# One chunk of 256 tokens instead of two of 128 in the chunked mLSTM of a three-block network

## The reference

```python
def mlstm_scan(q, k, v, li, lf, state):
    """true C = C*exp(m)."""
    ...
    def step(carry, inp):
        C, n, m = carry
        qx, kx, vx, lix, lfx = inp
        b = jnp.cumsum(lfx, axis=-1)
        dmat = b[..., :, None] - b[..., None, :] + lix[..., None, :]
        dmat = jnp.where(lower, dmat, -jnp.inf)
        inter = b + m[..., None]
        m_t = jnp.maximum(inter, jnp.max(dmat, axis=-1))
        w = jnp.exp(dmat - m_t[..., None])
        a = jnp.exp(inter - m_t)
        s = jnp.einsum("bhtd,bhsd->bhts", qx, kx) * w
        num = a[..., None] * jnp.einsum("bhtd,bhde->bhte", qx, C) + jnp.einsum("bhts,bhse->bhte", s, vx)
        den = a * jnp.einsum("bhtd,bhd->bht", qx, n) + jnp.sum(s, axis=-1)
        h = num / jnp.maximum(jnp.abs(den), jnp.exp(-m_t))[..., None]
        ...  # decay the state, add this chunk's keys times values
        return (C_new, n_new, m_new), h

def merge(y_fourier, h, o, g_f, g_m, head_g, w_four, w_mproj, w_out):
    hn = rmsnorm_2(h.transpose(0, 2, 1, 3), head_g.reshape(M_HEADS, M_HEAD_DIM)).reshape(B, T, M_WIDTH)
    hm = jax.nn.sigmoid(o) * hn
    y = jax.nn.sigmoid(g_f) * (y_fourier @ w_four) + jax.nn.sigmoid(g_m) * (hm @ w_mproj)
    return y @ w_out
```

## Time and profile before

| | us |
|---|---|
| median of 3 runs | 2546.47 (2544.3 to 2546.47) |
| the profiled execution | 2544.8, of it the span 2543.4 |
| TensorE busy | 2069.5 (81%) |
| DVE, ACT busy | 1008.2, 747.2 |
| the stage of the four heads | 1689 to 1886 |

### The profile page before, as it was taken

The page is one execution under the profiler, slowest core; times in us unless marked ns, Lnnn a source line. Parts: engine busy times, 40 slices in busy tenths (PEclk is TensorE's granted clock), DMA queues, the critical chain, the costliest instruction groups (busy, mean ns, idle before and its releaser), DMA issues.

```text
span 2543.4 us, 29602 instructions
## 1 busy us (share of the span) xinstructions
PE 2069.5 (81%) x12430; PEld 1378.3 (54%) x12430; DVE 1008.2 (40%) x1791; ACT 747.2 (29%) x1197; POOL 24.6 (1%) x21
## 2 busy tenths in 40 slices
PE   5888767777778787877688899778789899889895
PEld 3534313323333333323343798577778799676694
DVE  2533321112212212223442545665655545553475
ACT  4333320101111111122110444423344544533344
POOL 0000000000000000000000000000000000000000
PEclk8979888899898899888898999888889899899897
DMA  9848799999999999999999555152144455340430
GB/s 359 330 165 316 295 399 414 410 409 410 410 405 411 411 411 411 408 409 405 385 409 403 167 185 172 50 165 69 57 143 164 133 183 179 107 137 1 149 108 16
DMA packets 228243, 672.08 MB, mean 264 GB/s; under 512 B 11520, under 2 KB 134528, under 8 KB 187792
## 3 DMA queue, kind: packets, MB, share of 16 engines
q1 hardware_dynamic: 228112, 670.21, 69.3%
HBM read 669.12 MB, written 1.05 MB: 263 GB/s over the span
## 4 chain that ended last, share of the span: by engine, by line
PE 54%; DMA 28%; DVE 11%; ACT 5%; issue 2%; POOL 0%; SPq 0%; DVEq 0%; ACTq 0%
DMA ring<-in_w 22%; PE pb L227 12%; PE pb L228 12%; PE pb L229 12%; DMA ring<-in_w_a 3%; PE pb L1481 3%; PE pb L1504 2%; DVE WB L310 2%; PE pb L578 2%; DMA ring<-in_w_in 1%; DMA ring<-in_w_mod 1%; ACT WB L304 1%; PE pb L1465 1%; DVE tmpT L414 1%; PE pb L755 1%
## 5 line engine op out<-in xcount | busy, mean ns | idle before, releaser
L310 DVE TENSOR_TENSOR WB<-ring,WB 128x1024 fp32r<-128x1024 f32 (+3 forms) x370 | 425.2, 1191 | 506.3 <-ACT WB L304 505.8
L304 ACT ACTIVATE WB<-ring 128x1024 fp32r<-128x1024 f32 (+3 forms) x370 | 361.2, 1025 | 814.0 <-DMA ring<-in_w_a 466.8
L227 PE MATMUL pb<-HH,WB 128*128 128x256 f32 (+1 forms) x1680 | 504.3, 300 | 20.7 <-DVE big L2348 8.0
L228 PE MATMUL pb<-HL,WB 128*128 128x256 f32 (+1 forms) x1680 | 491.6, 293 | 0.0
L229 PE MATMUL pb<-HH,WB 128*128 128x256 f32 (+1 forms) x1680 | 490.8, 292 | 0.0
L1481 PE MATMUL pb<-ring,big 128*32 128x512 f32 x2048 | 300.1, 679 | 145.0 <-DMA ring<-in_w 127.7
L227 PEld LDWEIGHTS pb<-HH,WB 128*128 128x128 f32 x1680 | 338.0, 201 | 47.8 <-issue 20.7
L228 PEld LDWEIGHTS pb<-HL,WB 128*128 128x128 f32 x1680 | 337.9, 201 | 2.4 <-issue 2.2
L229 PEld LDWEIGHTS pb<-HH,WB 128*128 128x128 f32 x1680 | 336.9, 201 | 0.0
L1481 PEld LDWEIGHTS pb<-ring,big 128*32 128x32 f32 x2048 | 47.1, 114 | 365.6 <-DMA ring<-in_w 272.5
L1504 PE MATMUL pb<-ring,big 128*32 128x512 f32 x1024 | 174.2, 667 | 59.1 <-DMA ring<-in_w 51.0
(11 more groups left out here) (420 smaller groups left out, 2043.8 us busy)
## 6 DMA issues: line engine op xcount, KB each, us to landing
ring<-in_w SPq DMA_DIRECT2D x384, 1024.0 KB, 14.4
ring<-in_w_a SPq DMA_DIRECT2D x66, 1024.0 KB, 11.8
ring<-in_w_in SPq DMA_DIRECT2D x38, 1024.0 KB, 7.5
ring<-in_w_b SPq DMA_DIRECT2D x33, 1024.0 KB, 5.1
ring<-in_w_ada SPq DMA_DIRECT2D x32, 1024.0 KB, 6.3
ring<-in_w_mod SPq DMA_DIRECT2D x24, 1024.0 KB, 8.3
ring<-in_w_out SPq DMA_DIRECT2D x8, 1024.0 KB, 5.2
ring<-in_b_w_in SPq DMA_DIRECT2D x8, 1024.0 KB, 6.4
```

The lines of the kernel that those rows point to most:

```text
L227: pe.matmul(o, l[0], r[0], start=start, stop=False)
L228: pe.matmul(o, l[0], r[1], start=False, stop=False)
L304: act.activation(WB[:, c % 2, 0, x:y], flat[:, x:y], ACT.Copy).then_inc(*A(("high", c, z)))
L310: dve.tensor_tensor(WB[:, c % 2, 1, x:y], flat[:, x:y], WB[:, c % 2, 0, x:y].bitcast(F32), ALU.subtract).then_inc(*V(("low", c, z), *([("f ...
```

## The change

The 256 tokens of a head are one chunk. Per head the exponents of both directions are two matmuls of 36 rows and 256 columns (`M`), and two more (`A`) make the factor of the old state, which DVE multiplies into q (`qa`, two operations of 512 columns) ahead of the output matmuls. The scores (8 matmuls of 128x128) are made once and serve both directions: for the two blocks on the diagonal in both, and for the other two in one each. An output bank collects weighed scores times values and `qa` times the state as one sum in PSUM, 14 matmuls of 128x257 per head in four banks. Keys are no longer transposed or weighed, and the state isn't updated, decayed or kept. `finish` transposes into one bank in its third step instead of its fifth, there is one `hs` instead of two, and the denominators work straight from PSUM. `mlstm` has 6 steps instead of 8, and each is paired with 4 steps of `proj`. The silu of k stands ahead of the O units. In the gates, scans run over 256 tokens; the state's decay and the rows for it go.

Of the diff, the functions `mlstm` are shown by their new lines alone, since the old ones stand above.

```diff
+                    dve.tensor_tensor_scan(in_time(MM_c, d), in_time(rr_c, d), in_time(rr_c, d), 0.0, ALU.max, ALU.max).then_inc(*V())
+                dve.wait_ge(*last("v"))
+                for d in range(2):
+                    dve.tensor_tensor(small[seg[d], 0:1], at_end(bb_c, d), at_end(MM_c, d), ALU.add).then_inc(*V())
+                    dve.tensor_scalar(qw_c[seg[d], :], rr_c[seg[d], :], at_end(MM_c, d), None, ALU.subtract).then_inc(
+                        *V(*([("gate_rows_c",)] if d else [])))
...
         def gates_columns():
             q_ = gate_rows()
-            pe.wait_ge(*at("dd"))
-            pe.matmul(PB[2][:, 0:8], ones[0:36, :], q_[0][:, 0:8], start=True, stop=True).then_inc(*P(("dec",)))
+            pe.wait_ge(*at("gate_exps"))
             x = 0
-            for qi, ap in enumerate((q_[3], q_[6], q_[4], q_[5])):
...
         def finish(h):
-            for _ in range(4):
-                yield
+            yield
+            yield
             for i in range(2):
                 pe.wait_ge(*at("hs_gated", h, i))
-                pe.wait_ge(*(at("C", h + 1, 1, i) if h < 3 else at("hm_out", 2, i)))
+                if i == 0:
+                    pe.wait_ge(*at("wT", min(h + 1, 3)))
                 for f in range(2):
-                    e = pe.transpose(PB[6 + i][:, 128 * f:128 * f + 128], hs[h % 2][:, i, 128 * f:128 * f + 128], ident)
-                e.then_inc(*P(("hs_turned", h, i)))
-            yield
+                    e = pe.transpose(PB[3][:, 256 * f + 128 * i:256 * f + 128 * i + 128], hs[:, i, 128 * f:128 * f + 128], ident)
+            e.then_inc(*P(("hs_turned", h)))
 
...
         def mlstm(h):
             fin = finish(h - 1) if h else iter(())
+            q_, k_, v_ = qTm[h % 2], kTm[h % 2], va[h % 2]
+
+            def rows_of(d):
+                return k("m8")[0:36, 4 * d + h:4 * d + h + 1].to_broadcast([36, 128])
+
+            pe.wait_ge(*(at("hm_out", h - 2) if h >= 2 else at("gc_out")))
+            for d in range(2):
+                e = pe.matmul(PB[3][:, 256 * d:256 * d + 256], rows_of(d), MM[:, :], start=True, stop=True)
+            e.then_inc(*P(("M", h)))
+            pe.wait_ge(*(at("den", h - 1, 1, 1) if h else at("gc_out")))
+            for d in range(2):
+                e = pe.matmul(PB[4][:, 256 * d:256 * d + 256], rows_of(d), qA[:, :], start=True, stop=True)
+            e.then_inc(*P(("A", h)))
             pe.wait_ge(*at("ready", h))
+            for x, (s_, t) in enumerate(BLOCKS):
+                for f in range(2):
+                    e = pe.matmul(PB[2][:, 128 * x:128 * x + 128], k_[:, f, 128 * s_:128 * s_ + 128], q_[:, f, 128 * t:128 * t + 128],
+                                  start=f == 0, stop=f == 1)
+            e.then_inc(*P(("S", h)))
+            steps(fin, 1)
+            yield
+            steps(fin, 1)
+            yield
+            steps(fin, 1)
+            yield
+            for d in range(2):
+                for t in range(2):
+                    o = PB[OB[2 * d + t]][:, 0:257]
+                    if (d, t) == (0, 0):
+                        pe.wait_ge(*at("sT", h))
+                    if h:
+                        pe.wait_ge(*at("den", h - 1, d, t))
+                    elif (d, t) == (0, 1):
+                        pe.wait_ge(*at("y_low", 3))
+                    pe.matmul(o, wT[:, d, 128 * t:128 * t + 128], v_[:, t, :], start=True, stop=False)
+                    if t != d:
+                        pe.matmul(o, wT[:, d, 256:384], v_[:, d, :], start=False, stop=False)
+                    for f in range(2):
+                        e = pe.matmul(o, qa[:, f, d, 128 * t:128 * t + 128], Cc(h, d, f), start=False, stop=f == 1)
+                    e.then_inc(*P(("num", h, d, t)))
+                yield
+            yield
 
...
+            def silu(x, names):
+                x = x.rearrange("p a b -> p (a b)")
+                act.activation(x, x, ACT.Silu).then_inc(*A(*names))
+
...
         def mlstm(h):
             fin = finish(h - 1) if h else iter(())
+            steps(fin, 1)
+            yield
+            act.wait_ge(*at("wT0", h))
+            for d in range(2):
+                act.activation(wT[:, d, 256:384], PB[3][:, 256 * d + 128 * (1 - d):256 * d + 128 * (1 - d) + 128], ACT.Exp,
+                               bias=gc[:, 0, d, 4 * d + h:4 * d + h + 1], scale=-1.0).then_inc(*A())
+            for d in range(2):
+                for t in range(2):
+                    w = wT[:, d, 128 * t:128 * t + 128]
+                    act.activation(w, w, ACT.Exp, bias=gc[:, 0, t, 4 * d + h:4 * d + h + 1]).then_inc(*A(*([("wT", h)] if d and t else [])))
+            steps(fin, 1)
+            yield
+            steps(fin, 1)
+            for _ in range(4):
                 yield
...
+                dve.tensor_tensor_scan(in_time(MM, d), in_time(rr, d), in_time(rr, d), small[seg[d], 0:1], ALU.max, ALU.max).then_inc(*V())
+            dve.wait_ge(*last("v"))
+            for d in range(2):
+                s_ = seg[d]
+                dve.tensor_scalar(qA[s_, :], MM[s_, :], -1.0, small[s_, 0:1], ALU.mult, ALU.add).then_inc(*V())
+                dve.scalar_tensor_tensor(q_f[s_, :], bb[s_, :], -1.0, MM[s_, :], ALU.mult, ALU.subtract).then_inc(
+                    *V(*([("gate_rows",)] if d else [])))
+            yield
...
         def finish(h):
-            so, hs_ = sos[h % 2], hs[h % 2]
-            yield
+            so = sos[h % 2]
             dve_rstd(dve, ("hs", h), st[:, 52:54])
-            yield
             yield
             for i in range(2):
                 dve.wait_ge(*last("v"))
-                dve.scalar_tensor_tensor(hs_[:, i, :], hs_[:, i, :], st[:, 52 + i:53 + i], hg[:, 256 * h:256 * h + 256], ALU.mult, ALU.mult).then_inc(
+                dve.scalar_tensor_tensor(hs[:, i, :], hs[:, i, :], st[:, 52 + i:53 + i], hg[:, 256 * h:256 * h + 256], ALU.mult, ALU.mult).then_inc(
                     *V(*([("free", "hg")] if (h, i) == (3, 1) else [])))
                 dve.wait_ge(*at("so", h))
                 dve.wait_ge(*last("v"))
-                dve.tensor_tensor(hs_[:, i, :], hs_[:, i, :], so[:, i, :], ALU.mult).then_inc(*V(("hs_gated", h, i)))
-            yield
-            yield
-            for i in range(2):
-                src = PB[6 + i][:, 0:256].rearrange("p (f t) -> p f t", f=2)
-                x = (slice(None), slice(2 * h, 2 * h + 2), slice(256 + 128 * i, 384 + 128 * i))
-                dve.wait_ge(*at("hm_high", h, i))
-                dve.tensor_tensor(HL[x], src, HH[x].bitcast(F32), ALU.subtract).then_inc(*V(("hm_out", h, i)))
+                dve.tensor_tensor(hs[:, i, :], hs[:, i, :], so[:, i, :], ALU.mult).then_inc(*V(("hs_gated", h, i)))
+            yield
+            x = (slice(None), slice(2 * h, 2 * h + 2), slice(256, 512))
+            dve.wait_ge(*at("hm_high", h))
+            dve.tensor_tensor(HL[x], PB[3][:, :].rearrange("p (f t) -> p f t", f=2), HH[x].bitcast(F32), ALU.subtract).then_inc(
+                *V(("hm_out", h)))
 
...
         def mlstm(h):
             fin = finish(h - 1) if h else iter(())
+            q_ = qTm[h % 2]
+            yield
+            dve.wait_ge(*at("M", h))
+            dve.tensor_tensor(wT[:, :, 0:256].rearrange("p d (b t) -> p d b t", b=2), tri[:, :, None, :].to_broadcast([128, 2, 2, 128]),
+                              PB[3][:, :].rearrange("p (d b t) -> p d b t", d=2, b=2), ALU.subtract).then_inc(*V(("wT0", h)))
+            dve.wait_ge(*at("A", h))
+            for f in range(2):
+                dve.tensor_tensor(qa[:, f], q_[:, f, None, :].to_broadcast([128, 2, 256]), PB[4][:, :].rearrange("p (d t) -> p d t", d=2),
+                                  ALU.mult).then_inc(*V())
+            steps(fin, 1)
+            dve.wait_ge(*at("S", h))
+            dve.wait_ge(*at("wT", h))
+            w = wT[:, :, 0:256]
+            dve.scalar_tensor_tensor(w, PB[2][:, None, 0:256].to_broadcast([128, 2, 256]), 0.0625, w, ALU.mult, ALU.mult).then_inc(*V())
+            w = wT[:, :, 256:384]
+            dve.scalar_tensor_tensor(w, PB[2][:, 256:512].rearrange("p (d t) -> p d t", d=2), 0.0625, w, ALU.mult, ALU.mult).then_inc(*V(("sT", h)))
+            yield
+            steps(fin, 1)
+            yield
+            steps(fin, 1)
+            for d in range(2):
+                for t in range(2):
+                    o = PB[OB[2 * d + t]]
+                    dn = st[:, 48 + 2 * d + t:49 + 2 * d + t]
+                    dve.wait_ge(*at("num", h, d, t))
+                    dve.tensor_copy(dn, o[:, 256:257]).then_inc(*V())
                     dve.wait_ge(*last("v"))
+                    dve.scalar_tensor_tensor(dn, dn, -1.0, dn, ALU.mult, ALU.max).then_inc(*V())
                     dve.wait_ge(*last("v"))
+                    dve.tensor_scalar(dn, dn, gc[:, 1, t, 4 * d + h:4 * d + h + 1], None, ALU.max).then_inc(*V())
                     dve.wait_ge(*last("v"))
                     dve.reciprocal(dn, dn).then_inc(*V())
```

(58 more changed lines are left out.)

219 lines of the change are left out of this document (43 added, 176 removed).

## The result

The changed kernel takes 2502.34 us (median of 4 runs, 2499.35 to 2505.45) against 2546.47 before: ratio 0.9827, interval 0.981 to 0.9844, 44 us faster. The profiled execution took 2499.35 us (span 2498.0).

The account below looks back on a forecast made before the run. TensorE's work, waits and clock, not transfers, were taken to bound the heads. Gains 1.2 + 0 + 2.1 + 14.4 + 8.1 + 6.8 - 0.5 = 32.1 us turned the 2546.47 median into 2514.4, range 2504 to 2528.

Parts of the forecast that it names:

- context gates: Context part's gates: scans over 256 instead of 128 halve DVE's 4.4 us block; gain 1.2 us, bounds 0 and 2.3.
- latent gates: Latent's gate rows: key weight load leaves about 3.0 us later, 2.9 come back behind the split; net 0, bounds -2 and +1.
- gate columns: Ahead of the first mlstm matmul: `dd`, `dec`, half the small matmuls and copies go; gain 2.1 us, bounds 0 and 2.5.
- head 0: First latent head, 50.1 us before: 35.6 after, with no transposes of an earlier head; gain 14.4, bounds 10 and 16.
- head 1: Second latent head, 52.8 us before: 44.7 after, with one wait at the transposes; gain 8.1, bounds 4 and 12.
- head 2: Third latent head, 51.5 us before: 44.7 after, with one wait at the transposes; gain 6.8, bounds 4 and 12.
- head 3 and its end: Last head and `finish(3)`, 42.6 us before: denominator waits go, the last transposes' wait grows; 43.1, loss 0.5, bounds -3.5 and +3.
- a low phase as behind today's waits ... taken 3.4: Heads 1 and 2, behind the transposes' wait: 6.60 to 9.09 us at low clock, 0.44 lost each, 2.9 to 4.0 us.
- The price of a head's work at full clock: TensorE's matmuls in a head without waits: 33.8 us, 34.2 with issue, including 2.5 for the 8 scores.
- Rival (d): Wait at the transposes is shorter as ACT and DVE overlap more, low phase too: gain 38 to 44, 2505 us; chance 0.09.
- Rival (b): Clock also falls at each head's start, at small matmuls M, A, S: 4 us more in three heads, 2526 us; chance 0.14.
- rival (e): Clock stays at 0.50 from the transposes' wait to the end of heads 1 to 3: 20 us slower, 2566; chance 0.03.

Follow-up runs that it names:

- gating early: Changed kernel with the gating of the head before moved to the head's start on ACT and DVE, ahead of the split of K: 2486.38 us.
- transposes later: Changed kernel with only the transposes moved one unit later, behind Kf0: 2495.32 us.
- the fill of the kernel before: Kernel before with unread 128x256 matmuls ahead of the second chunk's scores, where TensorE waits for denominators: 2537.92 us, ratio 0.9965.
- the timed experiment: Kernel before with only the context part's gates run over 256 tokens at once: 2544.35 against 2546.46 us, ratio 0.9991.
- the two fill experiments: Unread matmuls put into TensorE's waits: changed kernel, before the transposes of heads 1 to 3, 2496.51 us; kernel before, before the second chunk's scores, 2537.92 us.

## Why the prediction missed its size

By its own steps, for the profiled pair (45.4 us in spans, 32.1 forecast):

| step | forecast | measured |
|---|---|---|
| context gates | 1.2 | 3.5 |
| latent gates | 0 | -0.1 |
| gate columns | 2.1 | 2.2 |
| head 0 | 14.4 | 15.7 |
| head 1 | 8.1 | 10.8 |
| head 2 | 6.8 | 10.0 |
| head 3 and its end | -0.5 | 3.3 |

**What held.** The mechanism, and where: no middle wait, the transposes as the one new wait, its length to 0.3 us, the order of DVE as its cause (gating early, transposes later), the broadcast forms at their lower bound (0.68 and 0.64 each). The latent gates give back what they lose: `conv` starts at 1667.50 instead of 1670.89, 3.4 earlier, where 3.5 had come from ahead. Of the signs named, heads 1 and 2 were outside theirs: 42.0 and 41.5 us at a clock of 0.92, not 43 to 47 at 0.85.

**What failed: "a low phase as behind today's waits ... taken 3.4".** That term of heads 1 and 2 was mis-sized. It measured 1.5 and 1.05 in the first profile, 2.5 in another, and 1.9 on average over three waits in the timed runs (5.8 us). The loss of 0.44 per low microsecond held: where the clock alone differs (heads 1 and 2 with early gating), 3.4 of them cost 1.5 us. Their number was wrong: 3.4 us are 7.7 low microseconds of work, and there were 4.07 and 3.09, since part of each stretch passes while TensorE stands. The two windows of the earlier trace rows don't both belong to a wait alone: the fill of the kernel before gives back 2.1 for a middle wait, and the longer one, at a head's start, comes also with a wait of 0.83. The price of a head's work at full clock was high by 0.8 (33.4 of work, 34.2 forecast), most of it in the 8 scores, 1.8 us (1719.76 to 1721.57) where 2.5 were taken. A slip besides: 50.1 less 35.6 is 14.5, not 14.4.

**What failed: head 3 "taken as 43.1".** The step weighed waits only. From M to the second half of the transposes, the window of 39.8 us (1843.43 to 1883.26) became 33.4 with 24 matmuls fewer in it (2.9 us), so 3.5 less for equal work, though its waits grew from 8.8 to 11.8. So some 6.5 us came from matmuls that are no longer there and from the clock; the step gave them no value. In that window TensorE worked 13.6 us at the low clock before (6.90, 6.04 and 0.69 behind its three waits) and 3.9 after (3.17 and 0.69). At 0.44 each that is an estimated 4.3 us for the clock, and 2.2 for the matmuls.

The same count for all four heads, an estimate too: to the second half of the last transposes they are 43 us shorter. TensorE worked 58.3 us at the low clock there before and 11.0 after, which makes 21 us; it stood 37.7 us before and 25.4 after, which makes 12. About 10 are matmuls at full clock, of which 2.9 only moved behind. The clock was the largest part of the gain, larger than the waits themselves.

**What was only bounded.** The context part: DVE's block fell by 2.1 as bounded. The single pair of profiles shows 3.5 for the stage, the timed experiment 2.1 with an interval that reaches 0. So the stage probably passed all of it on, where half had been assumed; the rest of the 3.5 is within the scatter.

Rival (d), 2505, was nearest in time and had 0.09, but by another mechanism: it had the low phase shorter because the wait is, and the wait was as forecast. Rival (b) didn't happen in the kernel after: at the M, A and S matmuls of its heads the clock stays full. It is true of the kernel before, where the clock also falls with waits of 0.8 us and less, so "without a wait ahead nothing forces the fall" was too strong. Each filled wait gave 1.9 to 2.1 us back in the two fill experiments. By the rule of the Trainium skill, page "TensorE: Matmul & The Clock Gate", section "HAM oscillation — how this bites in real kernels", that waits throttle the array, the runs agree for the filled waits. The slower rival (e) would have needed 32 low microseconds of work in a head; there were 4.1 at most in the profile after.

**Open.** Why the clock falls at the small matmuls of the old head starts, and not at the new ones, wasn't separated; they differ in shapes, number and spacing.

## What to carry to other kernels

When a stall goes, look for the instruction that is queued in order behind the next late result; here moving a 2 us gating to the head's start, ahead of the split, was worth another 16 us on top of the change's 44. Price a stage from all it executes, removed work and clock included, not from its waits alone; and price the slow clock by filling a wait with unused work, or by the slow microseconds in which the engine works, not by the length of slow stretches nearby. Undo a part before crediting it: the silu's place was worth 12 us in the old kernel and nothing beyond the scatter in the new one.

## What the runs showed of the hardware

Filling waits of 5.4 to 6 us with unused matmuls kept the clock of heads 1 and 2 at 1.00 where it was 0.92, and paid 1.9 us per wait. Two equal waits of 1.84 us (gating early, heads 1 and 2) had different ends: no low clock behind the first, 3.4 us of it behind the second. In the kernel before with the early silu, the clock was at 1.2 GHz behind a head's start although TensorE had stood for only 0.83 us there. And the same program reached one and the same place 7.4 us apart in two executions, nearly all of it lost in its first 300 us, so that a pair of profiles can't size an edit of 3 us.
